# Order of TensorE's products in a two-block transformer kernel: narrow rest products placed among the wide ones, and transposes placed one by one

## The reference, cut to what matters

```python
x = x + 0.5 * swiglu(rms_norm(x, ffn1_norm), ffn1_w_gate, ffn1_w_up, ffn1_w_down)
u = rms_norm(x, mix_norm) @ w_in
x = x + jnp.concatenate([f_out, a_out], axis=-1) @ w_out      # Fourier mixer, grouped attention
...
x = x + short_conv_mixer(h, conv_w_in[l], conv_w[l], conv_w_out[l])
...
s = jnp.einsum("bshd,bmhd->bhsm", q, k) * (MEM_HEAD_DIM ** -0.5)
p = jax.nn.softmax(s, axis=-1)
o = jnp.einsum("bhsm,bmhd->bshd", p, v).reshape(bsz, seq, D_MODEL)
return o @ w_o
```

## Time and profile before

| | |
|---|---|
| median of 3 runs | 1240.01 us (1239.48 to 1240.45) |
| the profiled execution: from first to last instruction | 1237.7 us |
| PE busy | 1229.1 us (99% of the span) |
| weight loads busy (PEld) | 1095.2 us (88%) |
| DVE busy | 928.1 us (75%) |
| ACT busy | 658.7 us (53%) |
| DMA, mean | 179 GB/s, 221.74 MB |
| mean granted TensorE clock | 0.999 of full speed |

### The profile page before, as it was taken

How to read it: one execution, slowest core, us unless ns; L and a number is a source line. 1 busy time by engine, 2 the same in 40 slices (tenths; PEclk the granted TensorE clock), 3 DMA queues, 4 the chain that set the end, 5 groups by cost and what they waited for, 6 DMA issues and landing times.

```text
span 1237.7 us, 18082 instructions
## 1 busy us (share of the span) xinstructions
PE 1229.1 (99%) x7432; PEld 1095.2 (88%) x7432; DVE 928.1 (75%) x1292; ACT 658.7 (53%) x872; POOL 31.1 (3%) x23
## 2 busy tenths in 40 slices
PE   9999999999999999999999999999999999999998
PEld 8888889978888888888888888889998888888887
DVE  7887866878777858988568777669968657877744
ACT  6655544456555444546546555445555445555632
POOL 0000000000000000440000000000000000000000
PEclk9999999999999999999999999999999999999999
DMA  9565664235555663556346555644445533555560
GB/s 329 187 213 177 224 209 164 75 137 172 187 186 188 214 216 131 186 188 211 130 138 233 188 190 186 222 170 152 156 142 182 187 136 137 204 200 177 198 209 34
DMA packets 51426, 221.74 MB, mean 179 GB/s; under 512 B 4464, under 2 KB 5776, under 8 KB 30864
## 3 DMA queue, kind: packets, MB, share of 16 engines
q1 hardware_dynamic: 51056, 220.25, 51.7%
q10 hardware_dynamic: 288, 0.33, 0.1%
HBM read 219.52 MB, written 1.05 MB: 178 GB/s over the span
## 4 chain that ended last, share of the span: by engine, by line
PE 92%; DVE 5%; issue 1%; DMA 1%; ACT 0%; SPq 0%; DVEq 0%; ACTq 0%
PE bank L418 48%; PE bank L462 21%; PE bank L422 7%; PE bank L449 5%; PE bank L507 2%; DVE wt L1271 2%; PE bank L761 2%; PE bank L789 2%; PE bank L484 1%; PE bank L510 1%; PE bank L489 1%; DMA raw<-weights 1%; PE bank L777 0%; PE bank L544 0%; DVE xn L1280 0%
## 5 line engine op out<-in xcount | busy, mean ns | idle before, releaser
L1271 DVE TENSOR_TENSOR wt<-raw,wt 128x2048 fp32r<-128x2048 f32 x202 | 464.1, 2299 | 67.8 <-ACT wt L916 67.4
L916 ACT ACTIVATE wt<-raw 128x2048 fp32r<-128x2048 f32 x202 | 386.0, 1911 | 119.7 <-PE bank L422 89.8
L418 PE MATMUL bank<-xn,wt 128*128 128x512 f32 x1712 | 416.3, 393 | 1.4 <-DVE scratch L1376 0.7
L418 PEld LDWEIGHTS bank<-xn,wt 128*128 128x128 f32 x1712 | 313.0, 188 | 63.0 <-DVE xn L1280 1.1
L418 PE MATMUL bank<-h,wt 128*128 128x512 f32 x1004 | 246.1, 392 | 0.0
L462 PEld LDWEIGHTS bank<-xn,wt 128*128 128x128 f32 x1824 | 234.3, 191 | 9.7 <-DVE wt L1271 0.8
L462 PE MATMUL bank<-xn,wt 128*128 128x256 f32 x1824 | 238.2, 283 | 0.2 <-DVE wt L1271 0.2
L418 PEld LDWEIGHTS bank<-h,wt 128*128 128x128 f32 x1004 | 182.5, 188 | 34.1 <-issue 0.4
L1376 DVE TENSOR_TENSOR scratch<-bank,rest 128x512 f32<-128x512 f32 x98 | 67.6, 690 | 86.9 <-ACT rest L928 86.8
L999 ACT ACTIVATE h<-scratch 128x256 fp32r<-128x256 f32 x88 | 36.8, 418 | 158.7 <-DVE scratch L1416 158.7
L928 ACT ACTIVATE rest<-bank 128x512 f32<-128x512 f32 x114 | 67.6, 593 | 65.9 <-PE bank L462 64.4
(11 more groups left out here) (227 smaller groups left out, 972.3 us busy)
## 6 DMA issues: line engine op xcount, KB each, us to landing
raw<-weights SPq DMA_DIRECT2D x158, 1024.0 KB, 4.9
raw<-weights SPq DMA_DIRECT2D x88, 512.0 KB, 4.9
raw<-weights SPq DMA_DIRECT2D x8, 256.0 KB, 4.5
k_t<-mem_t SPq DMA_DIRECT2D x2, 1024.0 KB, 8.1
raw<-weights SPq DMA_DIRECT2D x8, 128.0 KB, 4.1
out_t<-work SPq DMA_DIRECT2D x4, 256.0 KB, 2.3
x<-x_t SPq DMA_DIRECT2D x3, 256.0 KB, 5.3
v_s<-fourier SPq DMA_DIRECT2D x2, 256.0 KB, 5.3
```

The costliest lines, as they stand in the source:

```text
L418: return pe.matmul(out, hi, a.rearrange("p a s -> p (a s)"), start=first, stop=False, skip_group_check=True)
L916: act.activation(wt[t % RING][:, 0], raw[t % RING][:], ACT.Copy).then_inc(weight_hi, 1)
L1271: dve.tensor_tensor(wt[t % RING][:, 1], raw[t % RING][:], wt[t % RING][:, 0].bitcast(F32), ALU.subtract).then_inc(weight_lo, 1)
```

## The change

A new table `LAG` and a function `lag_of` say, for each tile, by how many contraction blocks k the narrow products follow the wide ones. In `square_tile` with a lag, the wide product of block (k, m) is followed by the narrow one of block (k - lag, m): first 2*lag wide ones, then wide and narrow in turn, then 2*lag narrow ones. The wait for `weight_lo` stands after 2*lag wide products instead of after all 16. A lag of 8 leaves a tile as it was. The inner `run` of `down` and `value_tile` are treated alike, without a table in the value tile. Tiles of `gu1` to `gu3` get a lag of 3 (the second tile 5, the first is unchanged), `gu0` 4, most `down` tiles 0, `conv_in` 8, then 6, then 4. The transposes are now handed to `pieces` as `between`: each of the four stands after one of the first four wide products of the piece that follows, and the scores that came behind them stand behind the fourth. In block attention the three transposes stay together ahead of the piece. One contraction block moves in `PIECES` from the second to the third piece of the first grouped pair.

```diff
+LAG = {**{(f"gu{n}", j): (4 if n == 0 else {1: 5}.get(j, 3)) for n in range(4) for j in range(14 if n == 0 else 7)},
+       **{(f"down{n}", i): 5 for n in range(4) for i in range(2)},
+       **{("conv_in", j): 8 if j < 6 else 6 if j < 9 else 4 for j in range(12)},
+       ("w_out", 2): 8, ("w_out", 3): 5, ("conv_out", 0): 4, ("conv_out", 1): 4, ("conv_out", 2): 6, ("conv_out", 3): 4,
+       ("mem_o0", 2): 6, ("mem_o0", 3): 4, ("mem_o1", 2): 6, ("mem_o1", 3): 4,
+       **{("moba_o", b): 2 for b in range(4)},
+       ("mem0", 1): 7, ("mem0", 2): 3, ("mem1", 1): 5, ("mem1", 2): 2}
+
+
+def lag_of(name, j, k0, k1):
+    return min(LAG.get((name, j), 2 if k1 < KB else 0), k1 - k0) if k0 == 0 else 0
...
-    "gqa": {0: ([(1, 0, 4)], [(1, 4, 7)], [(1, 7, 8), (2, 0, 2)]), 1: ([], [(2, 2, 6)], [(2, 6, 8), (3, 0, 1)]),
+    "gqa": {0: ([(1, 0, 4)], [(1, 4, 6)], [(1, 6, 8), (2, 0, 2)]), 1: ([], [(2, 2, 6)], [(2, 6, 8), (3, 0, 1)]),
...
                 w = wt[t % RING]
+                if lag is not None:
+                    if ks[0] == 0:
+                        pe.wait_ge(weight_hi, t + 1)
+                    for k in range(ks[0], ks[1] + lag):
+                        if k < ks[1] and ready is not None:
+                            for s, value in ready(k):
+                                pe.wait_ge(s, value)
+                        if k < ks[1] and k in beside:
+                            beside[k]()
+                        if ks[0] == 0 and k == lag:
+                            pe.wait_ge(weight_lo, t + 1)
+                        for m in range(ms):
+                            if k < ks[1]:
+                                with_hi(out[:, m, :], w[:, 0, m * KB + k, :], a[:, k], k == 0)
+                                if (k, m) in between:
+                                    between[k, m]()
+                            if k - lag >= ks[0]:
+                                mm = with_rest(out[:, m, :], w[:, 1, m * KB + k - lag, :], a[:, k - lag], k - lag == KB - 1)
+                    if ks[1] == KB:
+                        mm.then_inc(tile_done, 1)
+                    return
...
                     for n in range(NT):
                         pe.matmul(o[n], a[:, k, 0, tok[n]], w[:, :, :, k, :], start=k == 0, stop=False, skip_group_check=True)
-                for k in range(*ks):
-                    for n in range(NT):
+                        if (k, n) in between:
+                            between[k, n]()
                         mm = pe.matmul(o[n][:, 1], a[:, k, 1, tok[n]], w[:, 0, :, k, :], start=False, stop=k == KB - 1,
                                        skip_group_check=True)
...
+                                lag=None if in_parts or j == 0 else lag_of(phase, j, 0, KB),
...
+                    for n in range(len(blocks) + lag):
+                        if n < len(blocks):
+                            at, k, m, out = blocks[n]
+                            if k == FF - 1 and name in SHORT:
+                                pe.matmul(out[:, 0:S], w[:, 0, at, :], h[:, k, 0, :], start=False, stop=False, skip_group_check=True)
+                            else:
+                                with_hi(out, w[:, 0, at, :], h[:, k], k == 0)
+                        if n == lag and fresh:
+                            pe.wait_ge(weight_lo, t0 + i + 1)
+                        if n >= lag:
+                            at, k, m, out = blocks[n - lag]
+                            mm = with_rest(out, w[:, 1, at, :], h[:, k], k == final)
...
-                        mm = run(i, rows_at(0, range(4 * i, 4 * i + 4)), 0, range(4), True)
+                        mm = run(i, rows_at(0, range(4 * i, 4 * i + 4)), 0, range(4), True, lag=2 * LAG.get((name, i), 0))
...
+                for at, (j, k0, k1) in enumerate(PIECES[kind][n][i]):
+                    between = {(k0 + b // NT, b % NT): lambda b=b: turned(b) for b in range(NT * NT)} if turned and at == 0 else {}
...
                     pieces("gqa", p, 0, ready)
-                    turn(2 * p)
-                    if p < 3:
-                        grouped_scores(p + 1)
-                    pieces("gqa", p, 1, ready)
-                    turn(2 * p + 1)
-                    pieces("gqa", p, 2, ready)
+                    pieces("gqa", p, 1, ready, lambda b: turn(2 * p, b))
+                    pieces("gqa", p, 2, ready, lambda b: turn(2 * p + 1, b))
```

More of the change, by code:

```diff
@@ L422, in with_rest, with square_tile @@
                 return pe.matmul(out[:, S:2 * S], lo, a[:, 0, :], start=False, stop=last, skip_group_check=True)
-            def square_tile(t, out, a, ready=None, beside={}, lows=None, ks=(0, KB), ms=2, cuts=(), narrow=False, late=None):
+            def square_tile(t, out, a, ready=None, beside={}, lows=None, ks=(0, KB), ms=2, cuts=(), narrow=False, late=None, lag=None, between={}):
                 w = wt[t % RING]
+                if lag is not None:
[19 more added lines that the diff above has]
+                    return
                 for k0, k1 in zip((ks[0], *cuts), (*cuts, ks[1])):
@@ L491, in narrow_values, with value_tile @@
                     mm.then_inc(tile_done, 1)
-            def value_tile(t, out, a, beside={}, ks=(0, KB), narrow=False):
+            def value_tile(t, out, a, beside={}, ks=(0, KB), narrow=False, between={}):
                 w = wt[t % RING][:].rearrange("p a (m k) c -> p a m k c", m=2)
@@ L610, in rows_at, with run @@
                     return [(8 * half0 + 4 * n, k) for n, k in enumerate(ks)]
-                def run(i, rows, d, ms, fresh=False, final=None):
+                def run(i, rows, d, ms, fresh=False, final=None, lag=0):
                     w = wt[(t0 + i) % RING]
@@ L616, in run @@
                               for at, k in rows for m in ms]
[L617 to L627, removed]
+                    for n in range(len(blocks) + lag):
[10 more added lines that the diff above has]
+                            mm = with_rest(out, w[:, 1, at, :], h[:, k], k == final)
+                            if k == final and (d, m) in ((0, 1), (0, 3), (1, 1), (1, 2)):
+                                mm.then_inc(acc_done, 1)
                     return mm
@@ L772, in attention @@
                     pieces(kind, n, 0, ready)
[L773 to L782 removed]
+                    if a["causal"]:
+                        for b in (0, 2, 3):
+                            turn(n, b)
+                        pieces(kind, n, 1, ready)
+                    else:
+                        pieces(kind, n, 1, ready, lambda b: turn(n, b))
                     out_of(pe, kind, a["v_tile"])
```

61 lines of the change are left out of this document (34 added, 27 removed).

## The result

The changed kernel takes 1249.43 us (median of 4 runs, 1249.34 to 1249.56), the kernel before 1239.93 us beside it on the same chip (1239.48 to 1240.45). The ratio is 1.0077, with an interval of 1.0065 to 1.0089: slower by 9.5 us, where no change was forecast. The profiled execution has a span of 1247.8 us against 1237.7, so 10.1 us more.

A forecast was written before the change was run, and what follows sets the result against it. PE, busy for 1229.1 of 1237.7 us, was taken as the bound. The terms +2.1 - 2.3 + 0.2 + 0.2 + 0.1 = +0.3 us, added to the median, gave 1240.0 us; 8-in-10 range 1227 to 1246 us.

The forecast's parts named there:

- PE is the bound and there is nothing to win from waits: Whole kernel: PE is busy for 1229.1 of 1237.7 us, its longest wait is 1.0 us, so no idle time to win.
- The load behind a narrow product sticks out, so 340 ns is not to be had: Narrow slots: the next product's load sticks out some 7 ns; alternating, the following wide product bears it, 346.7 ns a pair.
- rival 1: A lone narrow product costs its columns alone, 340 ns a pair: 1221 to 1224 us, partly hidden 1229 to 1237; chance 0.36.
- A lone pair has 1 ns of surplus, with bounds of 0 and 4.3: 2,052 narrow products alone between wide ones: 1 ns each above 346.7 ns a pair, +2.1 us; bounds nothing and +8.8 us.
- the series: Surplus per cycle of sixteen, four, three and two wide and narrow products: 21, 16, 13, 7 ns; continued to one, 0 to 3.
- the 21 ns of surplus: Per tile, what sixteen wide and sixteen narrow products cost above steady slots; to be gone in `down2` tiles with lag 0.
- 114 fewer long changes of group, -2.3 us: Long changes from narrow to wide products fall from 207 to 93, at 21 ns each: -2.3 us.
- Transposes, +0.2 us, 0 to +1.0: 64 transposes one by one: 110 ns each kept, plus 0 to 15 ns for another load; taken as +0.2 us.
- Waits for `weight_lo`, +0.2 us: The earlier wait for DVE's split: tight only in `conv_in`, 0.1 us in its last tile; +0.2 us in all.
- The transposes' copy, +0.1 us: Grouped attention, ACT's copy: 0 to 0.2 us of waiting at each of two middle pairs, first pair's 0.6 us stays; +0.1 us.
- (2): Every lone pair pays a change of group, 2 to 4 ns or more: +4 to +9 us, 1242.6 to 1248 us; chance 0.24.

## Why the prediction was wrong, step by step

- **PE is the bound and there is nothing to win from waits.** Right: the waits went from 3.1 to 3.6 us and the loss is in PE's own slots.
- **The load behind a narrow product sticks out, so 340 ns is not to be had** (rival 1). Right. With 128 columns the slot still takes 112.1 ns in a group, and a lone pair 226.7 + 113.3; with 256 columns no stretch came below 346.7. Weight loads in the alternating stretch start with the product ahead of them, as in the earlier trace rows; the timeline of the changed kernel in `gu2` has a wide product and the load for the narrow one behind it:

```profile
705.15 0.40 PE L431 MATMUL bank<-xn,wt 128*128 128x512 f32 x1
...
705.16 0.19 PEld L435 LDWEIGHTS bank<-xn,wt 128*128 128x128 f32 x1
```

- **A lone pair has 1 ns of surplus, with bounds of 0 and 4.3.** This is the step that failed. It came from "Continued by the same step it is 0 to 3 ns" and from the upper bound "if a single pair paid as much per pair as a group of three". Measured: 0 in the cheap rhythm, 6.7 in the dear one, 5.5 in the mean over all lone products: +11.3 us where +2.1 stood, and above the +8.8 of the upper bound. With these 11.3 in the sum it comes to +9.5 instead of +0.3, on a span that grew by 10.1. What was wrong is that the price of a pattern was carried over from other patterns, and that it was taken to be one number. The reading at 10 ns was not what failed: the unrounded starts give 2.6 ns for the cycle of two and 10.6 for that of three where the prediction has 7 and 13, and continued from there the series gives nothing for a lone pair. That is what the cheap rhythm costs. That the same instructions have a second rhythm no row of the kernel before showed, and 6.7 ns lies above the price per pair of every cycle that the prediction read. In `down2`, where the 21 ns of surplus were to be gone, 143 pairs take 353.4 ns each.
- **114 fewer long changes of group, -2.3 us.** Right in kind and size: the version that alternates in the cheap rhythm wins 1.3 us for 79 of them, 16 ns each.
- **Transposes, +0.2 us, 0 to +1.0.** Right: 113 instead of 110 ns each, and 0.2 to 0.5 us for the whole.
- **Waits for `weight_lo`, +0.2 us.** Right in size (0.3 us, once), wrong in place. It came in `gu0`, not in `conv_in`, as the changed kernel's timeline shows (in brackets what PE waited for, and how long):

```profile
39.57 0.50 PE L431 MATMUL bank<-xn,wt 128*128 128x512 f32 x1 [0.26 <-DVE wt L1322]
```

- **The transposes' copy, +0.1 us.** Nothing came of it: PE waited for ACT's copy once, for 0.6 us, as before.
- **The rivals.** (2) came nearest: its condition (349 ns or more in `gu2`) was met at 353.3. But its price of 2 to 4 ns was taken from the same series, so the time of 1249.4 lies above both its 1248 and the range's 1246. Nor is the price one of each change of group, as it has it: some 300 lone pairs paid nothing, and a change between groups of two pays 3.4 ns.

What inside the engine makes two rhythms of one sequence stays open. Shown is that the entry into the stretch turns one into the other (1249.4 to 1244.6 us by one lag), that swapping the two banks does not, and that a narrow product of 128 columns has only one. Not shown is a rule for the entry: the number of pairs modulo 3 fell in one execution, three wide products ahead failed in `gu2` in another, and a wait of 2.2 us turned the rhythm from dear to cheap in one place, a pause of 0.1 us from cheap to dear in another.

## What to carry to other kernels

In a kernel whose TensorE is never idle, a new order of the same products is a new price list. Measure the very pattern, over a long stretch, before rewriting: a series over other patterns gave a bound that the real value passed. Judge such a kernel by the mean slot of each kind of product in a stage, and look for a second value of it in the same trace, since two stretches of one code can run in different rhythms. And where products alternate, the rest part has to be ready when its tile begins; in long groups its lateness is hidden, and slack must be read from the start of the tile.

## What the runs showed of the hardware that was not expected

- Alternating products of 512 and 256 columns, each with its own load, run at 346.7 or at 353.3 ns a pair, for hundreds of pairs without a change, and by what stood ahead of them. After an idle stretch of PE amid them, 0.1 to 2.2 us long, the other one can follow.
- A lone pair with 128 columns takes 340.0 ns, always the same; with 192 columns it takes 340.0 or 344.4.
- A product of 128 columns takes 112.1 ns in a group, and its first two slots behind a wide product are shorter; what they save is paid by the first wide product after the group.
